# A 512-token, two-layer hybrid model on one core: a reordered key search, gate slabs of sixteen keys, and part of a gate product moved from VectorE to ScalarE

## The chip, the cores and the metric

The kernel runs as one program on one core of a Trainium2 chip. The metric is the device time of an execution in microseconds; less is better. The kernel before was run three times.

## The reference, cut to what matters

The model has two layers over 512 tokens of width 1024 in float32. Each layer is a recurrent mixer, a cross attention and a product-key expert layer ("peer"). The change touches only the last:

```python
def block(hc):                       # D=1024, 8 heads, 2 x 128 keys, 16 chosen
    q = (hc @ wq).reshape(PEER_BLOCK, PEER_HEADS, 2, PEER_DHALF)
    sc = jnp.einsum('thcd,hckd->thck', q, keys)
    s1, i1 = lax.top_k(sc[:, :, 0], 16); s2, i2 = lax.top_k(sc[:, :, 1], 16)
    cand = (s1[..., :, None] + s2[..., None, :]).reshape(..., 256)
    cidx = (i1[..., :, None] * 128 + i2[..., None, :]).reshape(..., 256)
    top, pos = lax.top_k(cand, 16)
    eidx = jnp.take_along_axis(cidx, pos, axis=-1)
    gate = jax.nn.softmax(top, axis=-1)
    act = jax.nn.gelu(jnp.einsum('thkd,td->thk', u_tab[eidx], hc))
    return jnp.einsum('thk,thkd->td', gate * act, v_tab[eidx])
```

## The kernel before

The expert layer is computed densely for 352 tokens (TD) and by gathered rows for the other 160. Dense means: all 16384 experts are visited as 128 tiles of 128 experts. An up tile is 24 matmuls (8 slices of the width, each split into high and low parts and multiplied three times); its result, after gelu, goes to DRAM (`acts`) or stays in SBUF for the last 18 keys. A down tile is the gelu result times a gate matrix, then 24 more matmuls into 8 PSUM banks. TensorE takes the tiles in one fixed order. A tile m is loaded by a DMA that SyncE issues, its high part is made by ScalarE (`split_high`, L216), its low part by VectorE (`split_low`, L221); three tiles can be in flight (NRAW, NSPLIT), and SyncE's loop issues the load of a tile once the low part of the tile three before it is made.

Rows means: GpSimd gathers one expert row per token by indirect DMA (L2564, 128 rows of 4 KB, 0.52 MB), into a ring of six, and VectorE forms the dot product with the token (L2881) or, later, adds the weighted row of the down table (L2887). There are 160 gathers of the up table (ROWS) and 128 of the down table, with 32 more (`part_row`) summed by TensorE.

A layer's peer part has these stages, written out by hand as one program for each engine:
- Search. For each of eight heads VectorE runs `search` (top 16 of the key scores, top 16 of the pair sums `cand`, and the arithmetic that turns a position into two key numbers) while TensorE runs 12 tiles: two query tiles 512 wide and ten up tiles 352 wide, and 16 score matmuls. `split_and_row` puts one low part and, from the second head on, one or two dot rows between the steps of the search; 14 rows per head (ROWS_BY_HEAD). `link` makes VectorE wait for its own last instruction before it starts another.
- Groups. For each of 22 groups of 16 tokens VectorE makes two one-hot planes over the 128 keys (L2991, L2992) and three gate planes (L2994, the gate split into three bfloat16 parts), TensorE multiplies them (`spread_gates`, 48 matmuls, L2618), ScalarE copies the result (`take_gates`, L2737) and SyncE stores it to `gates` in DRAM. One or two up tiles stand between two groups. VectorE adds 0.75 dot rows per group (ROWS_BY_GROUP).
- The last 12 up tiles, with two dot rows each (ROWS_BY_TILE).
- Down. `weigh(e)` multiplies a gelu tile by its gates, which come back in slabs of 8 keys (1.4 MB, two buffers, one DMA each). What is left of the 160 dot rows is spread over the first 8 tiles (DOTS_UNTIL), and the 128 rows of the down table over tiles 10 to 124.

## Time and profile before

| | us |
|---|---|
| median of three runs (3557.41 to 3569.17) | 3567.39 |
| the profiled execution | 3566.76 |
| its span, first to last instruction | 3564.8 |

The share of the span that each engine is busy: TensorE 96%, VectorE 84%, ScalarE 38%, GpSimd 28%. TensorE's mean granted clock is 0.990 of full speed. In the rows below a time is in us from the span's start; a timeline row has start, duration, engine, line, operation, output<-inputs, and in brackets the idle time ahead of it with what ended it. The duration of an instruction on VectorE or ScalarE is longer than the distance to the next start where nothing has to be waited for. A row of busy times has the stretch, its length, then for each engine the busy time (and the number of instructions), and at its end the granted clock of TensorE, the share of DMA engines busy and GB/s.

### The profile page before, as it was taken

The numbers are of one execution on the slowest core, as the hardware profiler recorded it, in microseconds if no ns is written. First come the engines' busy times: TensorE is split into PE (matmuls) and PEld (weight loads), VectorE is DVE, ScalarE is ACT, GpSimd is POOL, SyncE is SP. The second block draws the span as 40 slices with busy tenths as digits, with TensorE's granted clock in tenths as the row PEclk, the third lists the DMA queues.
The fourth block names the chain that finished last, engine by engine and source line by source line (L and its number), as shares of the span: only waits on it lengthen the run. The fifth ranks groups of instructions, "written<-read, shape, count | busy, mean of one in ns | idle before, by whom it ended". The sixth has DMA issues, their size and how long they took to land. (4 is left out here: it accounts for less than half of the span.)

```text
span 3564.8 us, 68150 instructions
## 1 busy us (share of the span) xinstructions
PE 3416.0 (96%) x27550; PEld 3116.0 (87%) x27550; DVE 2986.1 (84%) x5697; ACT 1363.2 (38%) x2116; POOL 989.6 (28%) x756
## 2 busy tenths in 40 slices
PE   8899899999999989999999989999999999999998
PEld 5678677999899989999997877789998999999997
DVE  8687575899999978888888757489999997888887
ACT  3541343433334433333344135343333443333333
POOL 2000000133343245445510000002334324543452
PEclk9999999999999999999999999999999999999999
DMA  7820431699899999999962043259989999999995
GB/s 236 302 95 23 132 113 60 192 292 310 291 358 319 345 336 359 369 376 368 366 220 83 20 121 119 65 155 299 311 297 348 317 349 327 374 383 384 363 367 205
DMA packets 392170, 922.20 MB, mean 259 GB/s; under 512 B 33968, under 2 KB 211248, under 8 KB 385072
## 3 DMA queue, kind: packets, MB, share of 16 engines
q1 hardware_dynamic: 298672, 582.20, 48.7%
q0 software_dynamic: 93184, 335.65, 25.1%
q8 instruction: 217, 3.56, 0.4%
q14 instruction: 97, 0.79, 0.1%
HBM read 802.51 MB, written 113.05 MB: 257 GB/s over the span
## 5 line engine op out<-in xcount | busy, mean ns | idle before, releaser
L2564 POOL DMA_INDIRECT row<-in_peer_u_rows,row_at x320 | 414.6, 1296 | 739.0 <-DVE row L2881 629.3
L228 PE MATMUL peer_ps<-peer_h_high,tile_high 128*128 128x352 f32 (+1 forms) x1504 | 498.0, 331 | 17.0 <-DVE tile_low L221 14.1
L229 PE MATMUL peer_ps<-peer_h_low,tile_high 128*128 128x352 f32 (+1 forms) x1504 | 492.2, 327 | 0.0
L230 PE MATMUL peer_ps<-peer_h_high,tile_low 128*128 128x352 f32 (+1 forms) x1504 | 491.7, 327 | 0.0
L221 DVE TENSOR_TENSOR tile_low<-peer_tile,tile_high 128x1024 fp32r<-128x1024 f32 x362 | 441.4, 1220 | 30.9 <-ACT tile_high L216 27.4
L228 PE MATMUL peer_ps<-gate_high,tile_high 128*128 128x352 f32 x1360 | 442.6, 325 | 9.6 <-DVE tile_low L221 9.3
L230 PE MATMUL peer_ps<-gate_high,tile_low 128*128 128x352 f32 x1360 | 441.3, 325 | 0.0
L229 PE MATMUL peer_ps<-gate_low,tile_high 128*128 128x352 f32 x1360 | 439.5, 323 | 0.0
L216 ACT ACTIVATE tile_high<-peer_tile 128x1024 fp32r<-128x1024 f32 x362 | 379.5, 1049 | 14.1 <-DMA peer_tile<-in_peer_u 14.1
L216 ACT ACTIVATE gate_high<-weighed 128x352 fp32r<-128x352 f32 x256 | 127.8, 499 | 643.6 <-DMA peer_tile<-in_peer_v 332.6
L2881 DVE SCALAR_TENSOR_TENSOR row<-row,h_own 128x1024 f32<-128x1024 f32 x256 | 307.4, 1219 | 23.1 <-DMA row<-in_peer_u_rows,row_at 22.9
L2716 ACT ACTIVATE up_act<-peer_ps 128x352 f32<-128x352 f32 x220 | 102.5, 466 | 575.6 <-PE peer_ps L230 294.1
L228 PEld LDWEIGHTS peer_ps<-peer_h_high,tile_high 128*128 128x128 f32 x1504 | 282.7, 188 | 38.7 <-DVE tile_low L221 23.8
L2564 POOL DMA_INDIRECT late_row<-in_peer_v,row_at x130 | 223.5, 1719 | 239.6 <-DVE h_own L2887 221.1
L230 PEld LDWEIGHTS peer_ps<-peer_h_high,tile_low 128*128 128x128 f32 x1504 | 283.2, 188 | 3.9
L229 PEld LDWEIGHTS peer_ps<-peer_h_low,tile_high 128*128 128x128 f32 x1504 | 283.1, 188 | 3.9
L2564 POOL DMA_INDIRECT row<-in_peer_v,row_at x126 | 215.7, 1712 | 216.3 <-DVE h_own L2887 201.7
L228 PEld LDWEIGHTS peer_ps<-gate_high,tile_high 128*128 128x128 f32 x1360 | 255.3, 188 | 16.0 <-DVE tile_low L221 15.4
L228 PE MATMUL peer_ps<-peer_h_high,peer_tile_high 128*128 128x352 f32 (+1 forms) x736 | 249.9, 339 | 18.0 <-DVE peer_tile_low L221 12.4
L230 PEld LDWEIGHTS peer_ps<-gate_high,tile_low 128*128 128x128 f32 x1360 | 256.3, 188 | 0.0
L229 PEld LDWEIGHTS peer_ps<-gate_low,tile_high 128*128 128x128 f32 x1360 | 255.6, 188 | 0.0
L221 DVE TENSOR_TENSOR gate_low<-weighed,gate_high 128x352 fp32r<-128x352 f32 x256 | 133.0, 520 | 135.2 <-ACT tile_high L216 92.6
(571 smaller groups left out, 8179.0 us busy)
## 6 DMA issues: line engine op xcount, KB each, us to landing
peer_tile<-in_peer_u SPq DMA_DIRECT2D x256, 512.0 KB, 5.4
peer_tile<-in_peer_v SPq DMA_DIRECT2D x256, 512.0 KB, 6.2
gates<-gates_out SPq DMA_DIRECT2D x44, 1024.0 KB, 9.1
gates_in<-gates SPq DMA_DIRECT2D x32, 1408.0 KB, 10.4
acts<-up_act SPq DMA_DIRECT2D x220, 176.0 KB, 5.6
act_in<-acts SPq DMA_DIRECT2D x220, 176.0 KB, 6.1
in_w<-in_w_in SPq DMA_DIRECT2D x32, 512.0 KB, 3.6
peer_tile<-in_peer_wq SPq DMA_DIRECT2D x32, 512.0 KB, 5.1
```

Source lines behind the costliest of these rows:

```text
L216: return act.activation(out, value, ACT.Copy)
L221: return dve.tensor_tensor(out, value, high.bitcast(F32), ALU.subtract)
L228: pe.matmul(out, wh, mh, start=first, stop=False)
L229: pe.matmul(out, wh, ml, start=False, stop=False)
L230: return pe.matmul(out, wl, mh, start=False, stop=last)
L2564: pool.indirect_dma_start(row_of(n)[:, :], None, table, bass.IndirectOffsetOnAxis(ap=row_at[:, row_col(n):row_col(n) + 1], axis=0)) \
L2716: act.activation(up[i % NUP][:, :], ps[m % NPS][:, 0:TD], ACT.Gelu_apprx_tanh).then_inc(taken.sem, 1)
L2881: last = dve.scalar_tensor_tensor(out=x, in0=x, scalar=1.0, in1=(h_own if j < OWN else h_extra)[:, :], op0=ALU.mult, op1=ALU.mult, accum_o ...
```

## The change

- Search. The scans of a head are ordered so that low parts and rows stand behind almost every step: `mark` takes the number of an instruction, `gap` puts low parts and rows there (12 and 16 in 29 shares), and `until` waits for the marked one afterwards. Rows per head go from 14 to 16. The pair blocks become four of 16 pairs and one of a single pair (65 candidates for 64), and the number of a block is found by one shift by four bits, where there were one compare, three compare-and-adds and a cast.
- Groups. Of the third gate plane VectorE multiplies only the first four of eight token pairs (SCALED = 4); ScalarE makes the other eight tokens with eight instructions of 128 elements (`scale_third`), of which it does those of group g+1 between the tiles of group g and `take_gates(g)`, and those of group 0 ahead of both. `spread_gates` waits for them, and so does VectorE before it overwrites the second one-hot plane. Rows per group go from 0.75 to 1.25.
- The last 12 up tiles have one row each, where they had two.
- Slabs hold 16 keys, and are loaded in four pieces at different tiles; the first two loads take a half slab each. The second starts only in the down stage.
- GpSimd's order of gathers follows the new number of rows; its first gather of the down table also waits for the last gate store.

The diff, cut to its core (buffers' places and the counts of semaphores are left out):

```diff
+SCALED = 4
 OWN = PH * TOPK
 ROWS = OWN + PH * EX_COLS
 NROW = 6
 PARTS = 4
 EX_ROUNDS = PH * EX_COLS // PARTS
 BATCH = PH // 2
-ROWS_BY_HEAD, ROWS_BY_GROUP, ROWS_BY_TILE = 14, 0.75, 2.0
+ROWS_BY_HEAD, ROWS_BY_GROUP, ROWS_BY_TILE = 16, 1.25, 1.0
 DOTS_UNTIL = 8
 ROWS_END = NKEY - 4
-PAIRS = ((0, 1, 16), (1, 3, 8), (4, 4, 4), (8, 8, 1))
+PAIRS = ((0, 1, 16), (1, 2, 8), (3, 4, 4), (7, 8, 2), (15, 1, 1))
+GAPS = 29
 PAIR_AT = [sum(some * wide for _, some, wide in PAIRS[:j]) for j in range(len(PAIRS) + 1)]
 PAIRED = PAIR_AT[-1]
 SPILL = GROUP
-SLAB, NSLAB, NACT = 8, 2, 4
+SLAB, NSLAB, NACT = 16, 2, 4
 SLABS = NKEY // SLAB
-KEPT_LATE, KEPT_EARLY = SLAB, 10
+PIECES = ((0, 6), (6, 12), (12, 17), (17, TD // SPILL))
+KEPT_LATE, KEPT_EARLY = SLAB // 2, 10
 KEPT = KEPT_LATE + KEPT_EARLY
 NUP = 3
-DOWN = [s * SLAB + j for s in (*reversed(range(SLABS - -(-KEPT // SLAB), SLABS)), *range(SLABS - -(-KEPT // SLAB))) for j in range(SLAB)]
+TAKEN = [(SLABS - 1, SLAB // 2, SLAB // 2), (SLABS - 1, 0, SLAB // 2), *((s, 0, SLAB) for s in (SLABS - 2, *range(SLABS - 2)))]
+TAKEN_AT = [sum(some for _, _, some in TAKEN[:j]) for j in range(len(TAKEN))]
+DOWN = [s * SLAB + first + j for s, first, some in TAKEN for j in range(some)]
+PIECES_AT = [(0, 2, 4, 5), (4, 5, 6, 7), *([TAKEN_AT[s - 1] + 1 + j for j in ((2, 5, 8, 11) if TAKEN[s - 1][2] == SLAB else (0, 2, 4, 5))]
+                                           for s in range(2, len(TAKEN)))]
...
-PART_GATES_AT = (63, 105)
-PART_GATHER_AT = {42: 0, 79: 1, 88: 2, 96: 3, 108: 4, 111: 5, 114: 6, 117: 7}
+PART_GATES_AT = (71, 119)
+PART_GATHER_AT = {48: 0, 89: 1, 100: 2, 108: 3, 122: 4, 125: 5, 128: 6, 131: 7}
...
-            def load_slab(s):
+            def load_slab(s, piece):
                 if s >= NSLAB:
-                    sp.wait_ge(weighed.sem, weighed.at(SLAB * (s - NSLAB + 1)))
+                    sp.wait_ge(weighed.sem, weighed.at(TAKEN_AT[s - NSLAB + 1]))
+                elif s:
+                    sp.wait_ge(summed.sem, summed.at(UPS))
                 else:
                     for b in range(2):
                         sp.wait_ge(gates_stored[b].sem, gates_stored[b].at(16 * ((TD // SPILL + 1 - b) // 2)))
-                sp.dma_start(slabs[s % NSLAB][:, :, :], gates[DOWN[s * SLAB] // SLAB]) \
+                (at, first, some), groups = TAKEN[s], slice(*PIECES[piece])
+                sp.dma_start(slabs[s % NSLAB][:, groups, 0:some * SPILL], gates[at][:, groups, first * SPILL:(first + some) * SPILL]) \
                     .then_inc(slab_loaded[s % NSLAB].sem, 16)
 
             def load_act(e):
                     store(m - late)
                 if m in gates_at:
                     store_gates(gates_at[m])
-                if m == GROUP_AT[GROUPS] + late + 1:
-                    load_slab(0)
-                if m == UPS:
-                    load_slab(1)
+                if m - GROUP_AT[GROUPS] - late - 1 in PIECES_AT[0]:
+                    load_slab(0, PIECES_AT[0].index(m - GROUP_AT[GROUPS] - late - 1))
             for m in range(UPS + NRAW - late, UPS):
                 store(m)
             for e in range(NRAW, NKEY):
                 if FIRST_LOADED <= e + 2 and DOWN[e + 2:e + 3] and DOWN[e + 2] in LOADED:
                     load_act(LOADED.index(DOWN[e + 2]))
                 load(UPS + e)
-                s = (e - NRAW) // SLAB + NSLAB
-                if (e - NRAW) % SLAB == SLAB - 1 and s < SLABS:
-                    load_slab(s)
+                for s in range(1, len(TAKEN)):
+                    if e in PIECES_AT[s]:
+                        load_slab(s, PIECES_AT[s].index(e))
...
+                    for b in range(2):
+                        pool.wait_ge(gates_stored[b].sem, gates_stored[b].at(16 * ((TD // SPILL + 1 - b) // 2)))
...
+                pe.wait_ge(third_scaled.sem, third_scaled.at(g + 1))
...
+
+            def scale_third(g):
+                act.wait_ge(second_made.sem, second_made.at(g + 1))
+                for h in range(GROUP // 2 - SCALED, GROUP // 2):
+                    for t in range(2):
+                        token = g * GROUP + 2 * h + t
+                        last = act.activation(shares[g % 2][:, PLANES - 1, h, :, t], two[:, h, :, t], ACT.Copy, scale=left[:, token:token + 1])
+                last.then_inc(third_scaled.sem, 1)
...
+                if g == 0:
+                    scale_third(0)
+                if g + 1 < GROUPS:
+                    scale_third(g + 1)
...
-                lows(1)
+            def mark(ins):
+                vec_step.n += 1
+                ins.then_inc(vec_step.sem, 1)
+                return vec_step.n
+
+            def until(step):
+                dve.wait_ge(vec_step.sem, step)
+
+            def lows_of(hd):
+                return BRIDGE + 3 - (PH - 1 - hd) * (UPS_HEAD + 2) - slot_start[0]
+
+            def gap(hd, share):
+                gaps_done[0] += share
+                some = ROWS_BY_HEAD if hd else 0
+                both = (lows_of(hd) + some) * gaps_done[0] // GAPS
+                own_lows = min(both, (2 * lows_of(hd) * gaps_done[0] + GAPS) // (2 * GAPS))
+                lows(slot_start[0] + own_lows - done[0])
                 if hd:
-                    rows((hd - 1) * ROWS_BY_HEAD + ROWS_BY_HEAD * (done[0] - slot_start[0]) // (UPS_HEAD + 2))
-
-            def top16(some, hd):
+                    rows((hd - 1) * ROWS_BY_HEAD + both - own_lows)
+
+            def top16(some, hd, shares):
 
                 for x, r, v, a in some:
                     last = dve.max(v[:, 0:8], x)
-                link(last)
+                best_8 = mark(last)
+                gap(hd, shares[0])
+                until(best_8)
+                for x, r, v, a in some:
+                    last = dve.match_replace(out=r, in_to_replace=v[:, 0:8], in_values=x, imm_value=LOWEST)
+                replaced = mark(last)
                 for x, r, v, a in some:
                     dve.max_index(a[:, 0:8], v[:, 0:8], x)
-                    last = dve.match_replace(out=r, in_to_replace=v[:, 0:8], in_values=x, imm_value=LOWEST)
-                link(last)
-                split_and_row(hd)
+                gap(hd, shares[1])
...
+                gaps_done[0] = 0
                 for two_tb in range(2):
-                    top16([(sc[:, hd % 2, tb, x, :], rest[:, tb, x * NKEY:(x + 1) * NKEY], top[:, tb, x, :], at[:, tb, x, :])
-                           for tb in (2 * two_tb, 2 * two_tb + 1) for x in range(2)], hd)
-                    split_and_row(hd)
-                dve.sem_inc(searched.sem, 1)
+                    if two_tb:
+                        gap(hd, 1)
+                    keys_found = top16([(sc[:, hd % 2, tb, x, :], rest[:, tb, x * NKEY:(x + 1) * NKEY], top[:, tb, x, :], at[:, tb, x, :])
+                                        for tb in (2 * two_tb, 2 * two_tb + 1) for x in range(2)], hd, (2, 2, 2))
                 twins = lambda x: x.rearrange("p t (k a) -> p t k a", a=1).to_broadcast([P, TB, TOPK, 2])
-                dve.tensor_copy(at_first[:, :, :, :], twins(at[:, :, 0, :]))
-                dve.tensor_copy(payload[:, 1, :, :, :], twins(at[:, :, 1, :]))
                 at_pair = 0
                 for first, some, broad in PAIRS:
                     into = cand[:, :, at_pair:at_pair + some * broad].rearrange("p t (a b) -> p t a b", b=broad)
                     last = dve.tensor_tensor(into, down(top[:, :, 0, first:first + some], broad),
                                              across(top[:, :, 1, 0:broad], some), ALU.add)
                     at_pair += some * broad
-                link(last)
-                split_and_row(hd)
-                top16([(cand[:, tb, :], rest[:, tb, 0:PAIRED], best[:, tb, own], pos[:, tb, :])
-                       for tb in range(TB)], hd)
-                split_and_row(hd)
+                paired = mark(last)
+                until(keys_found)
+                dve.sem_inc(searched.sem, 1)
+                dve.tensor_copy(at_first[:, :, :, :], twins(at[:, :, 0, :]))
+                cast = mark(dve.tensor_copy(payload[:, 1, :, :, :], twins(at[:, :, 1, :])))
+                gap(hd, 1)
+                until(paired)
+                pairs_found = top16([(cand[:, tb, :], rest[:, tb, 0:PAIRED], best[:, tb, own], pos[:, tb, :])
+                                     for tb in range(TB)], hd, (2, 1, 2))
+                until(cast)
                 dve.tensor_tensor(payload[:, 0, :, 1:TOPK, :], at_first[:, :, 1:TOPK, :], at_first[:, :, 0:TOPK - 1, :], ALU.subtract)
-                link(dve.tensor_copy(spotf[0][:, :, :], pos[:, :, :]))
-                dve.tensor_copy(payload[:, 0, :, 0:1, :], at_first[:, :, 0:1, :])
-                link(dve.tensor_scalar(spotf[1][:, :, :], spotf[0][:, :, :], float(PAIR_AT[1]), None, ALU.is_ge))
-                link(dve.scalar_tensor_tensor(out=spotf[1][:, :, :], in0=spotf[0][:, :, :], scalar=float(PAIR_AT[2]),
-                                              in1=spotf[1][:, :, :], op0=ALU.is_ge, op1=ALU.add))
-                for _ in range(2):
-                    link(dve.scalar_tensor_tensor(out=spotf[1][:, :, :], in0=spotf[0][:, :, :], scalar=float(PAIR_AT[3]),
-                                                  in1=spotf[1][:, :, :], op0=ALU.is_ge, op1=ALU.add))
-                link(dve.tensor_copy(wide[:, :, :], spotf[1][:, :, :]))
-                link(dve.tensor_tensor(spot[:, :, :], mask[:, :, :], wide[:, :, :], ALU.logical_shift_right))
-                link(dve.tensor_tensor(spot[:, :, :], pos[:, :, :], spot[:, :, :], ALU.bitwise_and))
-                dve.tensor_copy(spotf[1][:, :, :], spot[:, :, :])
-                link(dve.tensor_tensor(hit[:, 0, :, :, :], across(spotf[0][:, :, :], TOPK), every(starts[:, :, :]), ALU.is_ge))
-                split_and_row(hd)
-                link(dve.tensor_tensor(hit[:, 1, :, :, :], across(spotf[1][:, :, :], TOPK), every(ranks[:, :, :]), ALU.is_equal))
+                steps_made = mark(dve.tensor_copy(payload[:, 0, :, 0:1, :], at_first[:, :, 0:1, :]))
+                until(pairs_found)
+                block_known = mark(dve.tensor_tensor(wide[:, :, :], pos[:, :, :], fours[:, :, :], ALU.logical_shift_right))
+                spot_0 = mark(dve.tensor_copy(spotf[0][:, :, :], pos[:, :, :]))
+                until(block_known)
+                masked = mark(dve.tensor_tensor(spot[:, :, :], mask[:, :, :], wide[:, :, :], ALU.logical_shift_right))
+                until(spot_0)
+                dve.tensor_tensor(hit[:, 0, :, :, :], across(spotf[0][:, :, :], TOPK), every(starts[:, :, :]), ALU.is_ge)
+                until(masked)
+                spot_1 = mark(dve.tensor_tensor(spot[:, :, :], pos[:, :, :], spot[:, :, :], ALU.bitwise_and))
+                gap(hd, 1)
+                until(spot_1)
+                spot_1 = mark(dve.tensor_copy(spotf[1][:, :, :], spot[:, :, :]))
+                gap(hd, 1)
+                until(spot_1)
+                hit_1 = mark(dve.tensor_tensor(hit[:, 1, :, :, :], across(spotf[1][:, :, :], TOPK), every(ranks[:, :, :]), ALU.is_equal))
+                gap(hd, 1)
+                until(hit_1)
                 pairs = hit[:, :, :, :, :].rearrange("p j t a (k c) -> p (j t a) k c", c=2)
-                link(dve.tensor_tensor(pairs, pairs, payload[:, :, :, :, :].rearrange("p j t (a k) c -> p (j t a) k c", k=1)
-                                       .to_broadcast([P, 2 * TB * TOPK, TOPK // 2, 2]), ALU.mult))
-                split_and_row(hd)
+                hits_known = mark(dve.tensor_tensor(pairs, pairs, payload[:, :, :, :, :].rearrange("p j t (a k) c -> p (j t a) k c", k=1)
+                                                    .to_broadcast([P, 2 * TB * TOPK, TOPK // 2, 2]), ALU.mult))
                 summed_hits = hit
                 for into in hits:
+                    gap(hd, 1)
...
+                    dve.wait_ge(third_scaled.sem, third_scaled.at(g))
+                dve.tensor_tensor(two[:, :, :, :], keys_at, per_key(1), ALU.is_equal).then_inc(second_made.sem, 1)
                 link(dve.tensor_tensor(one[g % 2][:, :, :, :], keys_at, per_key(0), ALU.is_equal))
                 for j in range(PLANES):
-                    last = dve.tensor_tensor(shares[g % 2][:, j, :, :, :], two[:, :, :, :], per_key(2 + j), ALU.mult)
+                    some = slice(0, GROUP // 2 - SCALED * (j + 1 == PLANES))
+                    last = dve.tensor_tensor(shares[g % 2][:, j, some, :, :], two[:, some, :, :], per_key(2 + j)[:, some, :, :], ALU.mult)
...
-                for _ in range(BRIDGE + 3 - (PH - 1 - hd) * (UPS_HEAD + 2) - done[0]):
-                    split_and_row(hd)
-                rows(hd * ROWS_BY_HEAD)
...
-                dve.wait_ge(slab_loaded[s % NSLAB].sem, slab_loaded[s % NSLAB].at(16 * (s // NSLAB + 1)))
+                dve.wait_ge(slab_loaded[s % NSLAB].sem, slab_loaded[s % NSLAB].at(16 * len(PIECES) * (s // NSLAB + 1)))
                 by = lambda x: x.rearrange("p (g t) -> p g t", t=SPILL)
                 dve.tensor_tensor(by(mixed[e % 2][:, :]), by(value),
-                                  slabs[s % NSLAB][:, :, (e % SLAB) * SPILL:(e % SLAB + 1) * SPILL], ALU.mult).then_inc(weighed.sem, 1)
+                                  slabs[s % NSLAB][:, :, (e - TAKEN_AT[s]) * SPILL:(e - TAKEN_AT[s] + 1) * SPILL], ALU.mult).then_inc(weighed.sem, 1)
...
```

## Rows read from the trace of the kernel before

**Rows 1.** The page's first section: busy time, share, instructions.

```profile
PE 3416.0 (96%) x27550; PEld 3116.0 (87%) x27550; DVE 2986.1 (84%) x5697; ACT 1363.2 (38%) x2116; POOL 989.6 (28%) x756
```

**Rows 2.** Busy time by stretch: search, groups, last up tiles, down; first and second layer.

```profile
691.00:1092.80 401.80, 390.42 (x2322) 367.74 (x2320) 381.15 (x1191) 142.88 (x206) 155.51 (x139) 1.00 0.92 314
1092.80:1273.40 180.60, 180.21 (x1809) 169.65 (x1809) 174.93 (x174) 84.21 (x146) 50.45 (x31) 1.00 1.00 324
1273.40:1333.50 60.10, 48.97 (x292) 47.81 (x289) 42.78 (x65) 18.76 (x29) 34.68 (x25) 0.96 0.97 357
1333.50:1420.00 86.50, 83.56 (x492) 81.54 (x492) 77.06 (x112) 30.06 (x44) 45.56 (x30) 0.97 0.97 362
1420.00:1851.00 431.00, 424.61 (x2614) 420.84 (x2613) 363.84 (x447) 159.91 (x221) 203.38 (x110) 1.00 0.93 349
...
2976.40:3035.50 59.10, 48.54 (x291) 47.67 (x288) 42.41 (x65) 18.49 (x29) 36.30 (x25) 0.97 0.97 364
3035.50:3120.00 84.50, 82.16 (x482) 80.67 (x483) 76.86 (x112) 29.64 (x43) 48.66 (x30) 0.96 0.99 372
3120.00:3546.70 426.70, 424.35 (x2624) 422.59 (x2622) 365.40 (x446) 157.34 (x218) 180.64 (x111) 1.00 0.92 350
```

**Rows 3.** The same view over 100 us in the middle of the second down stage.

```profile
3200.00:3300.00 100.00, 100.00 (x619) 100.00 (x619) 89.05 (x107) 37.57 (x52) 36.10 (x29) 1.00 1.00 382
```

**Rows 4.** Who waited for whom in 1273.4 to 1333.5: sum, times, longest.

```profile
DVE row L2881 <- DMA row<-in_peer_u_rows,row_at: 11.7, 9, 3.9
ACT tile_high L216 <- DMA peer_tile<-in_peer_u: 11.2, 4, 5.2
...
PE peer_ps L228 <- DVE peer_tile_low L221: 7.7, 2, 4.4
```

**Rows 5.** Timeline: the score matmuls of a head and two 512-wide matmuls on TensorE.

```profile
872.23 1.95 PE L2606 MATMUL peer_ps<-keys,queries 128*128 128x128 f32 x16
...
1852.67 0.39 PE L229 MATMUL front_ps<-front_x_low,front_tile_high 128*128 128x512 f32 x1
1852.90 0.40 PE L230 MATMUL front_ps<-front_x_high,front_tile_low 128*128 128x512 f32 x1
```

**Rows 6.** Timeline of VectorE: the first scans of two successive heads.

```profile
907.45 0.86 DVE L2849 MAX8 key_top<-key_scores 128x8 f32<-128x128 f32 x4
...
960.41 0.87 DVE L2849 MAX8 key_top<-key_scores 128x8 f32<-128x128 f32 x4
```

**Rows 7.** Timeline of VectorE: a step with a link behind it, then instructions without.

```profile
892.27 1.23 DVE L2931 TENSOR_TENSOR hit<-hit,pair_payload 128x2048 bf16<-128x2048 bf16 x1
893.53 1.23 DVE L221 TENSOR_TENSOR tile_low<-peer_tile,tile_high 128x1024 fp32r<-128x1024 f32 x1
894.68 1.22 DVE L2881 SCALAR_TENSOR_TENSOR row<-row,h_extra 128x1024 f32<-128x1024 f32 x1
```

**Rows 8.** Timeline of VectorE: first and last of the steps that find the block.

```profile
886.71 0.17 DVE L2917 TENSOR_SCALAR spotf<-spotf 128x64 bf16<-128x64 bf16 x1
...
887.92 0.23 DVE L2924 TENSOR_TENSOR spot<-pair_mask,pair_wide 128x64 uint32<-128x64 uint32 x1
```

**Rows 9.** VectorE, grouped by shape: a gate plane, and half its elements.

```profile
L2994 DVE TENSOR_TENSOR onehot_gates<-onehot_second,route 128x2048 bf16<-128x2048 bf16 x57 | 66.4, 1220 | 0.6
...
L2929 DVE TENSOR_TENSOR hit<-spotf,pair_ranks 128x1024 bf16<-128x1024 bf16 x8 | 5.5, 686 | 0.0
```

**Rows 10.** Timeline: TensorE's first gate product, and ScalarE around it.

```profile
1092.79 2.93 PE L2618 MATMUL peer_ps<-onehot_gates,onehot 128*128 128x128 bf16 x48 [0.86 <-DVE onehot_gates L2994]
...
1093.10 1.05 ACT L216 ACTIVATE tile_high<-peer_tile 128x1024 fp32r<-128x1024 f32 x1
1094.05 2.31 ACT L2737 ACTIVATE gates_out<-peer_ps 128x512 f32<-128x512 f32 x4
```

**Rows 11.** Timeline of ScalarE: an instruction of 128 elements.

```profile
1368.23 0.31 ACT L2815 ACTIVATE row_dots<-row_dots 128x128 f32<-128x128 f32 x1 [3.53 <-DVEq L3121]
```

**Rows 12.** Timeline: one of TensorE's waits in the down stage.

```profile
1446.93 0.43 PE L228 MATMUL peer_ps<-gate_high,peer_tile_high 128*128 128x352 f32 x1 [1.37 <-DVE peer_tile_low L221]
```

49 lines of the change are left out of this document (30 added, 19 removed).

## The prediction

> **What bounds the kernel now.** I read the page's first section, then the busy times by stretch, then the waits, then single timelines. TensorE is busy 96% of the span [rows 1], so all that can be won is the time in which it is held up, and a stretch where it is not held up gives nothing, whatever the other engines do. The busy times by stretch say where it is held up [rows 2]: idle TensorE is 401.8 - 390.4 = 11.4 us in the search, 0.4 us in the groups, 11.1 us in the last twelve up tiles, 2.9 and 6.4 us in the down stage. The second layer has about the same. A busy TensorE can still be slow, so I also set up floors. Where nothing disturbs it, 100 us hold 620 matmuls of 352 columns (619 are recorded) [rows 3], 0.161 us each, 3.86 us a tile.
> - Last up tiles: 12 x 3.86 = 46.4 us against 60.1 and 59.1 us. Lost: 13.7 and 12.7.
> - Down: 3072 x 0.1613 = 495.5, and some 3 us for the last small products, say 499, against 86.5 + 431.0 = 517.5 and 84.5 + 426.7 = 511.2. Lost: 18.5 and 12.2.
> - Search, per head: 240 x 0.16 = 38.4, the two query tiles 48 x 0.23 = 11.0, the scores about 1.8 [rows 5], so 51.2 us. The distance of two heads on VectorE is 52.96 us [rows 6], and the whole stretch has 11.4 us of idleness. Lost: about 12, in each layer.
> - Groups: nothing lost. VectorE is busy 174.9 of 180.6 us beside it, so two engines are full at once.
> Together 44 and 37 us, 81 us for both layers: no version of this change can win more.
>
> **What holds it up.** In the search VectorE is busy 381 of 402 us [rows 2]: it is the bound, and low parts come late behind long runs of scans. In the last up tiles it is the transfers: VectorE waits 11.7 us for gathered rows, ScalarE 11.2 us for up tiles, and TensorE then for low parts [rows 4]. The bytes say why: 12 tiles and 24 rows of 0.52 MB, two slabs of 1.44 and a gate store of 1.05 are 22.8 MB; at the floor's 46.4 us that is 490 GB/s, and the stretch moved 357 to 364 [rows 2]. In the down stage single waits of about 1 us come at about the pace of the slab loads [rows 12].
>
> **The change part by part.** The sum is made against the profiled execution's 3566.8 us (span 3564.8 and 2.0 around it), which lies 0.6 us below the median of the runs.
>
> Search. A linked step costs more than its work: the row after a link starts 1.26 us after a 1.23 us instruction, while two instructions without a link are 1.15 us apart, one of 1.23 and one of 1.22 us [rows 7]; so a link costs 0.11 us. A head has 29 links. Five go with the removed steps, and of the other 24 about 22 get a low part, a row or an independent step between, as 28 items are spread over 29 shares: 22 x 0.11 = 2.4 us. The removed steps run from 886.71 to 887.92, 1.2 us with their links [rows 8]. The shift and the fifth pair block come in, at about 0.13 us each (a 0.23 us step less what overlaps) 0.3 us. Two more rows cost 2 x 1.145 = 2.3 us. VectorE per head: -2.4 -1.2 +0.3 +2.3 = -1.0 us, to 51.9, close above TensorE's 51.2. Seven heads have rows, so 7 us; the first head, without new rows, is bound by TensorE. Even spacing of the low parts should take some of the single waits away, yet two more gathers per head add 1.05 MB in 53 us, 20 GB/s, to the 314 that the search moves with its DMA engines busy 0.92 [rows 2]. I take 6 us gained per layer; the bounds are 10 (nearly all that is lost, the floor binding) and a loss of 4 (as with the last up tiles, the late transfers return as waits).
> The Trainium skill, page "VectorE: DVE Perf Modes", section "Rules for kernel authors", says that chained VectorE instructions drain in any case, so that one should cut their number and not their semaphores. These rows differ from it: 1.26 against 1.15 us. By the page the 2.4 us would not come, VectorE would have 1.4 us more per head, and the search would lose about 10 us a layer.
>
> Groups. VectorE saves half a plane: 1.22 - 0.69 = 0.53 us per group [rows 9], 11.7 us in 22. It gains 27 - 16 = 11 rows, 12.6 us. Net +0.9 us, on an engine that has 5.7 us of room over the stage [rows 2]: hidden. If that room were gone it would cost the 0.9. ScalarE gets eight instructions of 128 elements, 0.31 us each alone [rows 11] and about 0.2 apart, 1.7 us a group; the upper bound is that they overlap in nothing and cost as a 352-wide one, 0.5 us, 4 us a group. ScalarE is busy 84.2 of 180.6 us, 3.8 of 8.2 per group, so 1.7 fits. Behind `scale_third` in its queue stand `take_gates` and the next tile's high part; the wait for the second plane is short, since that plane is VectorE's first step of the group and ends 4.6 us ahead of the last. One place has no cover: in group 0 `scale_third(0)` stands after the tile's high part, which ends at about 1094.05, while TensorE's first product now starts at 1092.79 after 0.86 us of waiting [rows 10]. It would start at 1094.05 + 1.7 = 1095.8: 3.0 us lost per layer (bounds 2 and 5). VectorE's wait for the same instructions before group 1 costs it some 2 us, which are covered by TensorE's own delay. Bigger stores (1 KB pieces for 512 B) and 11 more gathers stand against each other on DMA engines that are full here (1.00) [rows 2]; I take zero, from -1 to +2.
> The same skill, page "ScalarE: Activation LUTs", section "What ACT_TABLE_LOAD costs", gives about 93 ns more for an operand that is a pointer per partition, as this scale is. No row here has one of that form alone. By it the eight cost 2.5 us, and the first product comes 0.8 us later still.
>
> Last up tiles. 12 rows less, 6.3 MB, and the second slab's 1.44 MB go out: 22.8 - 7.7 = 15.1 MB in 46.4 us are 325 GB/s, below the 357 to 364 that the stretch has moved and below 382 [rows 3]. So the stage falls to its floor, with 2 us left: 11.7 and 10.7 gained (bounds 7, half of it, and all 13). The last piece of the first slab is issued for tile 144, two tiles or 7.7 us before VectorE wants it, about as long as a landing under load; VectorE's own lead over TensorE of some 4 us is the cover, and without it 1 to 2 us would be lost.
>
> Down, first 20 tiles. 160 - 142 = 18 dot rows are left before, 2.25 a tile; after, 98 + 14 + 4 + 27 + 12 = 155 are done and five are left. VectorE per tile goes from 0.44 + 0.44 + 1.14 + 2.25 x 1.145 = 4.6 us, above TensorE's 3.86, to 2.7. The loss there is 2.9 us of idleness and 0.03 x 86.5 = 2.6 us of clock at a granted 0.97 [rows 2]; I take 4 gained of these 5.5 (bounds 2 and 5). The second slab's last piece comes in tile 7 and is wanted for weigh(8), again two tiles.
> Down, the rest. The bytes are the same; bursts of 1.44 MB become pieces of 0.65 to 0.79 MB every three tiles. The idle time is 6.4 us in the first layer and 2.4 in the second [rows 2]. I take 3 and 1 (bounds 0, and all of it).
>
> Sum. First layer: 6 - 3 + 11.7 + 4 + 3 = 21.7. Second: 6 - 3 + 10.7 + 4 + 1 = 18.7. Together 40.4 us: 3566.8 - 40.4 = **3526.4**, and 3527 against the median.
>
> **The rivals.**
> A. The search is bound by transfers. For it: a DMA share of 0.92 already [rows 2]. Against it: the last down stage ran at 382 GB/s with TensorE full [rows 3]. It loses 4 us per layer instead of gaining 6: 3526 + 20 = 3546.
> B. The last up tiles are not freed, since pieces of the slab and the two small slack times take over: half of the gain, 2 x 5.6 = 11, and down tiles give 2 x 2 less: 3541.
> C. Links cost nothing, so that only the number of steps counts (the first skill rule). The search loses 10 instead of gaining 6: 3526 + 32 = 3558. Against it stands the 0.11 us of [rows 7].
> D. Slower: ScalarE becomes the bound of the groups. In a group with one tile TensorE needs 3.9 + 2.8 = 6.7 us; ScalarE needs 1.3 for the tile, 2.0 for the copies [rows 10] and eight scalings. From 0.42 us per scaling on it is the later one in 14 of 22 groups, and `spread_gates` waits each time; at 0.6 us it is 1.5 us x 14 = 21, with the waits for gate stores that its idle time now absorbs some 30 us a layer: 3526 + 60 = 3586. It decides against the change from about 0.55 us on. The 0.31 us row speaks against it [rows 11].
> E. More than forecast: the search reaches its floor and the down stage loses no more: 3526 - 2 x 4 - 7 = 3511.
>
> **How the numbers follow.** Forecast 0.50, A 0.14, B 0.11, C 0.07, D 0.07, E 0.11. The forecast's own range, with its bounds combined, is 3512 to 3543. To hold 8 in 10 the range takes in B, most of E and most of A with their bounds: 3502 to 3555. A measurement of this kernel can tell about 0.3%, 11 us, from no change. Faster by more than that (below 3556.7) are the forecast, B, E and four fifths of A: 0.83. The same: 0.10, from C and the end of A. Slower: 0.07, D.
>
> **What would show it.** The groups' stretch grows by 3 us, with one TensorE wait for ScalarE at its start, and no such wait in later groups. The last up tiles take 47 to 50 us, and VectorE's waits for gathered rows are gone there. The head distance on VectorE is 52 us or less, with 16 rows in it. The scalings last 0.3 to 0.4 us each. DMA in the search is at 335 to 345 GB/s. It would be wrong if ScalarE's waits for stores of `acts` reach TensorE in the search, or if the down stage's first ten tiles wait for slab pieces.

## The result, and the profile after

The changed kernel takes 3526.5 us (median of four runs, 3523.3 to 3528.3) where the kernel before, run beside it, takes 3564.4: a ratio of 0.989, 95% interval 0.987 to 0.991. The forecast was 3527, faster. Yet only the sum was right: several of its terms were off by about their own size or more, and the errors cancelled. That the total came out within 2 us is luck. So the experiments ask of each term whether its mechanism is there and what it is worth.

The span of the profiled execution is 3525.9 us (3564.8 before). These are the changed kernel's busy times by stretch, in the columns of [rows 2], each stretch beginning with TensorE's same instruction: first to last score product of the first layer (a part of the next line's stretch); search and the way to the first gate product; groups, last twelve up tiles and down stage of the first layer, then the last two stages of the second layer.

```profile
647.40:978.90 331.50, 327.75 (x1945) 311.40 (x1944) 315.87 (x1065) 124.20 (x180) 121.50 (x105) 1.00 0.88 300
690.00:1099.90 409.90, 395.75 (x2356) 374.70 (x2355) 380.91 (x1200) 148.87 (x218) 178.70 (x154) 0.99 0.94 330
1099.90:1284.00 184.10, 182.13 (x1809) 171.56 (x1810) 175.78 (x196) 130.91 (x313) 64.30 (x42) 0.99 0.94 337
1284.00:1330.30 46.30, 46.30 (x289) 46.30 (x289) 30.68 (x43) 18.10 (x28) 15.10 (x12) 1.00 0.97 354
1330.30:1831.60 501.30, 501.07 (x3105) 500.69 (x3103) 428.64 (x529) 189.91 (x264) 173.39 (x128) 1.00 0.93 349
2959.90:3006.20 46.30, 46.30 (x290) 46.30 (x289) 30.58 (x43) 18.29 (x28) 15.86 (x12) 1.00 0.97 352
3006.20:3507.30 501.10, 500.95 (x3105) 500.76 (x3104) 428.00 (x528) 186.85 (x260) 160.48 (x128) 1.00 0.93 348
```

The last up tiles and the down stage are at their floors in both layers: TensorE (second and third number) is busy with hardly a gap. The groups are longer than the 180.6 of [rows 2] although ScalarE (fifth number) has taken work from VectorE. And the way to the first gate product (second line) is longer than the 401.8 of [rows 2], where the forecast had it shorter.

To see where, I took the starts of the same TensorE instructions in both traces: the eight score products of a layer, the first gate product, the end of the groups, the first down tile. Times in us, first / second layer; every experiment was read in the same way.

| kernel | first to last score | to first gate product | groups | last up tiles | down |
|---|---|---|---|---|---|
| before | 338.6 / 336.9 | 111.4 / 113.0 | 180.8 / 180.5 | 59.9 / 59.0 | 517.5 / 510.8 |
| after | 331.5 / 331.3 | 121.0 / 118.8 | 184.0 / 185.8 | 46.3 / 46.3 | 501.2 / 501.0 |
| difference | -7.1 / -5.6 | +9.6 / +5.8 | +3.2 / +5.3 | -13.6 / -12.7 | -16.3 / -9.8 |
| after, run again | 328.5 / 329.2 | 119.8 / 120.7 | 184.4 / 183.4 | 46.3 / 46.3 | 501.0 / 501.0 |

The differences add up to -24.2 and -17.0, -41.2 us in all. The spans differ by 38.9, since the rest of the program is 2.3 longer: the first score product, ahead of which nothing is changed, starts at 647.4 and not at 642.8, and over all kernels here between 638.8 and 647.4. In the two executions of the changed kernel the first three columns differ by up to 3 us, the last two by 0.2.

Where TensorE now waits, by the view of its waits over the whole span (us in total, times, longest):

```profile
PE peer_ps L2631 <- ACT onehot_gates L2759: 11.1, 2, 6.0
PE peer_ps L228 <- ACT up_act L2729: 9.7, 12, 1.7
PE peer_ps L2631 <- DVE onehot_gates L3056: 4.9, 2, 3.0
PE peer_ps L228 <- DVE peer_tile_low L221: 4.8, 2, 3.0
```

The first row is ScalarE's scaling in group 0, once a layer, and is new. The second is TensorE waiting for ScalarE's activations in the search; the kernel before has such waits too:

```profile
PE peer_ps L228 <- ACT up_act L2716: 7.3, 6, 2.1
```

The third is a VectorE wait in the middle of the groups, once a layer. The fourth comes just ahead of group 0.

### The profile page after: what moved, and what is told of

Read it like the earlier page. It is cut to its first block and busy times, and to the rows that moved or that the text cites. A ratio compares the mean times of both kernels' runs of the same rounds, so it can differ in the third digit from the quotient of the medians.

```text
span 3525.9 us, 68362 instructions
## 1 busy us (share of the span) xinstructions
PE 3398.6 (96%) x27550; PEld 3112.3 (88%) x27550; DVE 2928.4 (83%) x5651; ACT 1463.5 (42%) x2468; POOL 877.6 (25%) x756
## 5 line engine op out<-in xcount | busy, mean ns | idle before, releaser
L2576 POOL DMA_INDIRECT row<-in_peer_u_rows,row_at x320 | 403.9, 1262 | 564.7 <-DVE row L2927 437.2
L228 PEld LDWEIGHTS peer_ps<-peer_h_high,tile_high 128*128 128x128 f32 x1504 | 282.7, 188 | 30.5 <-issue 18.7
L229 PE MATMUL peer_ps<-peer_h_low,peer_tile_high 128*128 128x352 f32 (+1 forms) x736 | 244.8, 333 | 0.0
L230 PE MATMUL peer_ps<-peer_h_high,peer_tile_low 128*128 128x352 f32 (+1 forms) x736 | 244.5, 332 | 0.0
```

What stands on the lines that cost most here:

```text
L228: pe.matmul(out, wh, mh, start=first, stop=False)
L229: pe.matmul(out, wh, ml, start=False, stop=False)
L230: return pe.matmul(out, wl, mh, start=False, stop=last)
L2576: pool.indirect_dma_start(row_of(n)[:, :], None, table, bass.IndirectOffsetOnAxis(ap=row_at[:, row_col(n):row_col(n) + 1], axis=0)) \
```

## The experiments

All ratios are to the kernel before on the same chip, with 95% intervals.

**The changed kernel again**, to have it beside the others.

> The changed kernel unchanged, as the mark for the other kernels of this set: both theories expect 0.989 of the kernel before, some 38 us less.

3522.9 us, ratio 0.988 [0.985, 0.991].

**The waits between linked steps put back.** The order of the search stays as it is.

```diff
                 ins.then_inc(vec_step.sem, 1)
+                dve.wait_ge(vec_step.sem, vec_step.n)
                 return vec_step.n
```

> The changed kernel, but every marked step of the search is waited for at once, as a link does, with order, rows and slabs as in the changed kernel. Theory: a wait for the last instruction costs 0.11 us, some 22 to 24 per head, 2.5 us a head on a VectorE that is the bound: the distance of two heads grows from about 52.5 to 54 or 55 us and the kernel is 20 to 35 us slower than the changed one. Rival (the rule that waits cost nothing and only the number of instructions counts): within 4 us of the changed one.

3560.2 us, 0.999 [0.997, 1.000]: nearly the whole gain is gone, 37 us of it against the changed kernel run again, a little more than the 20 to 35 expected. First to last score takes 347.1 / 344.1 us, 15.6 and 12.8 more than after (18.6 and 14.9 against its second execution). The first two of the seven distances from score to score, 16.7 and 51.1 us, are the same in both kernels, so all of it falls in the other five. VectorE's first scans of successive heads, from the second head on, stand 3.0 and 2.6 us further apart on average. The way to the first gate product grows by another 4 to 5. TensorE waits for VectorE's low parts again, as the view of its waits over the whole span says (the changed kernel has 1.8 us of this row, in 4 waits):

```profile
PE peer_ps L228 <- DVE tile_low L221: 26.4, 22, 2.4
```

So a wait of VectorE for its own last instruction is not free: 2.6 to 3.0 us for the 27 marks of a head are 0.10 to 0.11 us each, the forecast's 0.11 (it had counted 22 such waits). Rival C falls. With it, for this kernel, falls the rule of the Trainium skill, page "VectorE: DVE Perf Modes", section "Rules for kernel authors", by which one should cut the number of chained instructions and not their semaphores: here the number stayed and the semaphores cost 37 us.

**Rows put back, the rest of the change kept**, and **rows alone moved in the kernel before**. The part gates and part gathers that go with the rows are moved too.

```diff
-ROWS_BY_HEAD, ROWS_BY_GROUP, ROWS_BY_TILE = 16, 1.25, 1.0
+ROWS_BY_HEAD, ROWS_BY_GROUP, ROWS_BY_TILE = 14, 0.75, 2.0
...
-PART_GATES_AT = (71, 119)
-PART_GATHER_AT = {48: 0, 89: 1, 100: 2, 108: 3, 122: 4, 125: 5, 128: 6, 131: 7}
+PART_GATES_AT = (63, 105)
+PART_GATHER_AT = {42: 0, 79: 1, 88: 2, 96: 3, 108: 4, 111: 5, 114: 6, 117: 7}
```

The second kernel is the opposite edit in the kernel before.

> The changed kernel, but with the rows spread as before: 14 per head, 0.75 per group, 2 per last up tile, and GpSimd's part gathers at the places that go with it. Theory: the stalls of the last up tiles and of the first down tiles came from the transfers of 24 and 18 rows there, so the last twelve tiles go from 46.3 back to 56 to 60 us with VectorE waiting for gathered rows, the down stage from 501 to 504 to 508, while search and groups win some 4 us a layer: 20 to 35 us slower than the changed kernel. Rival: the slab pieces and their places freed these stages: the last up tiles stay below 50 us and the time within 8 us of the changed one.

> The kernel before, with nothing of the change but the spread of the rows (16, 1.25, 1) and the part gathers' places. Theory: the last up tiles fall to 47 us as in the changed kernel, but two more rows per head (2.3 us) and 11 more in the groups (12.6 us) fall on a VectorE without room, so search and groups grow by about 13 and 7 us a layer and eat the gain: 0.995 to 1.006 of the kernel before. Rival: the spread alone brings most of the change's gain, below 0.993.

Rows back: 3551.5 us, 0.996 [0.995, 0.998], within the 20 to 35 us expected. Rows alone: 3570.8 us, 1.001 [1.000, 1.002], as expected.

| kernel | first to last score | to first gate product | groups | last up tiles | down |
|---|---|---|---|---|---|
| rows back | 325.9 / 325.7 | 117.2 / 115.5 | 182.2 / 181.8 | 60.1 / 59.5 | 516.1 / 513.0 |
| rows alone | 347.8 / 346.5 | 116.4 / 116.9 | 190.7 / 193.9 | 46.0 / 46.3 | 504.0 / 502.5 |

The stretches from first to last score, last up tiles and down of rows back:

```profile
645.40:971.30 325.90, 325.84 (x1946) 311.55 (x1945) 304.86 (x1046) 124.02 (x180) 115.99 (x96) 1.00 0.85 288
1270.70:1330.80 60.10, 48.71 (x289) 47.55 (x287) 42.27 (x64) 18.10 (x29) 32.69 (x25) 0.95 0.96 344
1330.80:1846.90 516.10, 506.54 (x3104) 505.19 (x3104) 445.07 (x558) 190.00 (x264) 178.08 (x140) 0.99 0.94 353
```

and of rows alone, the groups, last up tiles and down:

```profile
1110.60:1301.30 190.70, 182.86 (x1809) 171.41 (x1810) 187.34 (x196) 84.10 (x145) 68.19 (x42) 0.99 0.99 327
1301.30:1347.30 46.00, 46.00 (x289) 46.00 (x289) 29.05 (x41) 18.36 (x28) 17.25 (x12) 1.00 1.03 396
1347.30:1851.30 504.00, 501.99 (x3106) 500.66 (x3104) 430.27 (x530) 190.24 (x265) 184.34 (x128) 1.00 0.92 345
```

Three readings. The 13 us stall of the last up tiles follows the rows alone: it returns with two rows per tile although the slab comes in pieces, and goes with one row although whole slabs stay. The new search order with 14 rows has TensorE busy 325.84 of 325.90 us, its floor; it is worth 12.7 and 11.2 us. The two added rows per head then cost 5.6 us a layer (2.6 and 3.5 if the second execution of the changed kernel is taken); in the old order they cost 9.2 and 9.6. And rows alone give nothing: what they free late (13.9 and 12.7 in the last up tiles, 13.5 and 8.3 in the down stage) they cost early (14 and 14 to the first gate product, 10 and 13 in the groups). The new search order makes them payable; what the scalings add is asked below. The down stage of rows back is worse than the 504 to 508 expected: nearly all of its loss, 15.0 us in the first layer, falls in its first 50 us, against 6.6 us there in the kernel before.

What the two rows cost in the search shows in ScalarE's waits there, the changed kernel first, from first to last score:

```profile
ACT up_act L2729 <- DMA acts<-up_act: 91.6, 28, 6.4
```

and rows back:

```profile
ACT up_act L2729 <- DMA acts<-up_act: 47.1, 12, 6.0
```

With the new order, ScalarE waits about twice as long for the buffers that the stores of `acts` give back, and some of it reaches TensorE: of the 5.6 us, TensorE's idle time is 3.7, and 3.1 of it waits for ScalarE's activations. But the number of rows alone does not set these waits. The kernel before, with 14 rows and the old order, has

```profile
ACT up_act L2716 <- DMA acts<-up_act: 84.5, 26, 6.6
```

DMA moves 300 GB/s in that stretch of the changed kernel, 288 in rows back, at a share of 0.88 and 0.85. So the DMA engines are not full on average; I read it as stores landing later among more gathers, but no run separates that from another cause.

**Group 0 left to VectorE.** ScalarE's scalings begin with group 1.

```diff
-                pe.wait_ge(third_scaled.sem, third_scaled.at(g + 1))
+                if g:
+                    pe.wait_ge(third_scaled.sem, third_scaled.at(g))
...
-                if g == 0:
-                    scale_third(0)
...
-                    dve.wait_ge(third_scaled.sem, third_scaled.at(g))
+                if g >= 2:
+                    dve.wait_ge(third_scaled.sem, third_scaled.at(g - 1))
...
-                    some = slice(0, GROUP // 2 - SCALED * (j + 1 == PLANES))
+                    some = slice(0, GROUP // 2 - SCALED * (j + 1 == PLANES and g > 0))
```

> The changed kernel, but VectorE makes the whole third plane of group 0, and TensorE, VectorE and ScalarE wait for scalings from group 1 on. Theory: the one uncovered place of the moved work is group 0, where TensorE waits 5.1 and 6.0 us for ScalarE and then runs at a lower granted clock; without it these waits fall below 1 us, the first gate product starts 5 us earlier, and the kernel is 10 to 16 us faster than the changed one (5 to 6 us and about 2 us of clock per layer). Rival: VectorE is as late as ScalarE there, so the wait only changes its name, and less than 4 us are won.

3513.1 us, 0.984 [0.981, 0.987], 10 us below the changed kernel, at the lower end of the 10 to 16 expected. The way to the first gate product is 114.4 / 115.9, 6.6 and 2.9 us less (5.4 and 4.8 against the second execution); the groups take 186.0 / 186.6.

How eight short instructions come to cost more than the 3.0 us of the forecast is seen in the changed kernel's timeline (start, us, engine, line, operation; in brackets the wait just before and what ended it):

```profile
1076.49 1.23 DVE L2927 SCALAR_TENSOR_TENSOR row<-row,h_extra 128x1024 f32<-128x1024 f32 x1 [3.15 <-DMA row<-in_peer_u_rows,row_at]
1085.27 0.43 PE L228 MATMUL peer_ps<-peer_h_high,peer_tile_high 128*128 128x352 f32 x1 [2.96 <-DVE peer_tile_low L221]
1093.63 0.47 ACT L2729 ACTIVATE up_act<-peer_ps 128x352 f32<-128x352 f32 x1 [9.88 <-DMA acts<-up_act]
1097.30 2.47 ACT L2759 ACTIVATE onehot_gates<-onehot_second,gates_left 128x128 bf16<-128x128 bf16 x8
1099.87 1.23 DVE L3052 TENSOR_TENSOR onehot_second<-key_ramp,route 128x2048 bf16<-128x2048 bf16 x1 [5.08 <-ACT onehot_gates L2759]
1099.91 4.57 PE L2631 MATMUL peer_ps<-onehot_gates,onehot 128*128 128x128 bf16 x48 [5.11 <-ACT onehot_gates L2759]
```

VectorE waits 3.15 us for a gathered row, low parts come late and TensorE waits 2.96; ScalarE has waited 9.88 us for a store of `acts` when it makes its last activation; only behind that come the eight scalings, at 1097.30, and they last 2.47 us, not 1.7. TensorE waits 5.11 us and VectorE 5.08. A late activation alone is not what the forecast missed, for the kernel before has it in the same place:

```profile
1091.20 0.46 ACT L2716 ACTIVATE up_act<-peer_ps 128x352 f32<-128x352 f32 x1 [6.86 <-DMA acts<-up_act]
```

Counted from the moment when TensorE has done its tiles (1091.93 before, 1094.80 after), the forecast's scalings would begin 2.1 us later and last 1.7, a wait of 3.8. Here they begin 2.5 us later and the product follows after another 2.6: 5.1. In the second layer they begin 3.4 us later, and the wait is 6.0:

```profile
2774.12 5.28 PE L2631 MATMUL peer_ps<-onehot_gates,onehot 128*128 128x128 bf16 x48 [6.01 <-ACT onehot_gates L2759]
```

Behind these waits the 48 products take 4.57 and 5.28 us, where they took 2.93 and 2.92 before: 1.6 and 2.4 us more, which the table counts among the groups. In the same place the kernel without group 0's scalings:

```profile
1088.42 2.47 ACT L2760 ACTIVATE onehot_gates<-onehot_second,gates_left 128x128 bf16<-128x128 bf16 x8
1086.36 2.92 PE L2632 MATMUL peer_ps<-onehot_gates,onehot 128*128 128x128 bf16 x48
1207.53 4.50 PE L2632 MATMUL peer_ps<-onehot_gates,onehot 128*128 128x128 bf16 x48 [2.66 <-DVE onehot_gates L3056]
```

The first gate product starts with no wait (1.03 us in the second layer), and the scalings (of group 1 now) run beside it. The third line is the VectorE wait in the middle of the groups: it stays, is longer than the changed kernel's 1.96, and the products behind it are slow now. That is why the groups do not get shorter although their first product does.

**The whole third plane on VectorE**, in every group, with rows and all else as changed.

```diff
-SCALED = 4
+SCALED = 0
...
-                pe.wait_ge(third_scaled.sem, third_scaled.at(g + 1))
...
-                if g == 0:
-                    scale_third(0)
-                if g + 1 < GROUPS:
-                    scale_third(g + 1)
...
-                    dve.wait_ge(third_scaled.sem, third_scaled.at(g))
```

> The changed kernel, but VectorE makes the whole third plane of every group, and nobody waits for ScalarE's scalings. Theory: VectorE gets 0.57 us per group, 12 us a layer, with some 5 us of room, so the groups grow to 188 to 192 us from their first product on while the wait of 5 us ahead of it is gone: 0 to 8 us slower than the changed kernel and 10 to 18 slower than group0_on_vector. Rival: VectorE has the room after all, the offload brings nothing, and the kernel is as fast as group0_on_vector.

3524.0 us, 0.988 [0.986, 0.991]: the time can't be told from the changed kernel's, and is 11 us above group 0 alone on VectorE, both as expected. The first gate product comes 5.0 and 2.2 us sooner (116.0 / 116.6), and the groups are longer by 8.2 and 3.9:

```profile
1085.70:1277.90 192.20, 182.54 (x1809) 171.11 (x1810) 187.38 (x196) 84.37 (x146) 67.13 (x42) 0.99 0.94 324
```

VectorE is busy 187.4 of 192.2 us: it is the bound. With the results above this makes a square for the groups, first / second layer:

| | plane on VectorE | half of it on ScalarE |
|---|---|---|
| 0.75 rows a group | 180.8 / 180.5 (before) | 182.2 / 181.8 (rows back) |
| 1.25 rows a group | 192.2 / 189.7 (this), 190.7 / 193.9 (rows alone) | 184.0 / 185.8 (after) |

At 0.75 rows the scalings only lose, 1.4 us, which is the slower products behind group 0's wait (4.92 and 4.48 us there); beside the added rows they give 4 to 8. (The kernels of a line differ in search order and slabs as well, which end or begin outside the groups; slabs of 16 keys are also stored in larger pieces within them, and no run takes that apart.) The 10 us of group 0 take about all of it back. So as written the scalings bring nothing, and the changed kernel's whole gain is there without them; begun with group 1 they do bring something.

**The scaling without its pointer operand.** The half of the third plane that ScalarE makes is copied and not multiplied.

```diff
-                        last = act.activation(shares[g % 2][:, PLANES - 1, h, :, t], two[:, h, :, t], ACT.Copy, scale=left[:, token:token + 1])
+                        last = act.activation(shares[g % 2][:, PLANES - 1, h, :, t], two[:, h, :, t], ACT.Copy, scale=1.0)
```

> The changed kernel, but ScalarE's eight scalings multiply by the constant 1.0 and not by the token's remainder of the gate, so this part of the gates is wrong; everything else is done. It is there for the price of the operand. The forecast's sum (from a 128-element instruction of 0.31 us) expects the same duration with the per-partition operand as without; the Trainium skill's page ScalarE: Activation LUTs expects about 0.09 us less per instruction here, so eight of them 1.8 us where the changed kernel shows 2.47.

Groups of instructions by line and form, in a stretch of the groups; the changed kernel first (shape, count, busy, mean ns of one, idle time before them and its cause), then this one:

```profile
L2759 ACT ACTIVATE onehot_gates<-onehot_second,gates_left 128x128 bf16<-128x128 bf16 x149 | 46.3, 430 | 8.2 <-DVE onehot_second L3052 8.2
```

```profile
L2759 ACT ACTIVATE onehot_gates<-onehot_second 128x128 bf16<-128x128 bf16 x144 | 31.4, 342 | 6.8 <-DVE onehot_second L3052 6.8
```

430 against 342 ns: the pointer costs 88 ns. The Trainium skill, page "ScalarE: Activation LUTs", section "What ACT_TABLE_LOAD costs", says about 93 for each such operand; the trace agrees. From it the prediction had estimated 2.5 us for eight, and they take 2.47, against 1.75 to 1.78 here (1.8 expected). The row that I had used is of float32 elements and a constant scale [rows 11]. The kernel's time, 3525.5 in its only run, can't be told from the changed kernel's.

**Whole slabs.** A slab of sixteen keys is loaded at once, two halves first.

```diff
-PIECES = ((0, 6), (6, 12), (12, 17), (17, TD // SPILL))
+PIECES = ((0, TD // SPILL),)
...
-PIECES_AT = [(0, 2, 4, 5), (4, 5, 6, 7), *([TAKEN_AT[s - 1] + 1 + j for j in ((2, 5, 8, 11) if TAKEN[s - 1][2] == SLAB else (0, 2, 4, 5))]
+PIECES_AT = [(0,), (4,), *([TAKEN_AT[s - 1] + 1 + j for j in ((2,) if TAKEN[s - 1][2] == SLAB else (0,))]
```

> The changed kernel, but each slab of gates comes in one transfer (1.4 MB for the two half slabs, 2.9 MB for the others), issued where the first piece was. Theory: the waits at slab loads in the down stage before came from bursts, so with bursts twice the size the down stage goes from 501 us to 508 to 515 and the kernel is 10 to 25 us slower than the changed one. Rival: the down stage was freed by the rows that are gone from its start, and a transfer asked for this early disturbs nobody: within 4 us.

3557.4 us, 0.998 [0.996, 0.999]: with whole slabs nearly all of the gain is gone, 31 to 35 us where 10 to 25 were expected, since the last up tiles suffer as well. Last up tiles and down stage of the first layer, by stretch, then the new wait of TensorE in the last up tiles, and ScalarE's wait for an up tile ahead of it (us in total, times, longest):

```profile
1281.20:1335.10 53.90, 48.62 (x289) 48.34 (x289) 30.41 (x43) 17.91 (x28) 16.61 (x12) 0.94 0.86 305
1335.10:1846.10 511.00, 503.66 (x3105) 500.41 (x3104) 427.63 (x529) 189.92 (x264) 194.26 (x128) 1.00 0.92 343
```

```profile
1317.44 0.66 PE L228 MATMUL peer_ps<-peer_h_high,tile_high 128*128 128x352 f32 x1 [5.28 <-DVE tile_low L221]
ACT tile_high L216 <- DMA peer_tile<-in_peer_u: 10.1, 1, 10.1
```

7.6 and 5.2 us come back in the last up tiles, 9.8 and 10.6 in the down stage. DMA moves 343 GB/s here and 349 in the changed kernel's down stage, so it is not the bytes. It is single tiles that come late: ScalarE's longest wait for an up tile in the last up tiles is 10.1 us, 0.6 in the changed kernel, and for a down tile 9.0 against 5.7. With sixteen-key slabs the pieces carry these 33 us. In the kernel with rows alone, where slabs hold eight keys and come whole, the last up tiles are free and the down stage loses only 3.0 and 1.5 us to the 501. So the pieces mostly pay for what the larger slab would cost; against whole slabs of eight keys, larger slabs and pieces together have 4.5 us to win in these stages.

**Three mends together.** Group 0 on VectorE, the last low parts of the search ahead of the rows, and one of GpSimd's part gathers three rows later, away from the wait of VectorE in the middle of the groups.

```diff
-PART_GATHER_AT = {48: 0, 89: 1, 100: 2, 108: 3, 122: 4, 125: 5, 128: 6, 131: 7}
+PART_GATHER_AT = {48: 0, 89: 1, 100: 2, 108: 3, 122: 4, 125: 5, 128: 6, 134: 7}
...
+            lows(1)
+            rows(searched_rows + 2)
+            lows(1)
             rows(searched_rows + 4)
             dve.wait_ge(flip_taken.sem, flip_taken.at(TB - 1))
-            lows(2)
```

> The changed kernel with three changes: group 0's third plane on VectorE; the two low parts ahead of the gate flips are made between and before the four rows there; the last gather of part rows stands ahead of row 134, where it stood ahead of row 131. Theory: the first saves 6 to 8 us a layer, the second the waits of 3.0 and 1.9 us with the clock behind them, 2 to 4 a layer, the third the waits of 2.0 and 3.0 us at the gate product of the fifteenth group: 20 to 28 us in all, near 3502. Rival: the transfers of acts set the pace there, and a mended wait returns a few us later: less than 14 us.

3510.7 us, 0.983 [0.979, 0.987], against 0.984 with group 0 alone: the other two give nothing that can be told. It is 12 us below the changed kernel, not 20 to 28; the rival had said less than 14. The wait that the moved gather was to remove, in the changed kernel's timeline:

```profile
1197.71 1.89 POOL L2550 DMA_INDIRECT part_row<-in_peer_v,row_at  x1 [14.74 <-PE peer_ps L2641]
1205.73 1.44 POOL L2576 DMA_INDIRECT row<-in_peer_u_rows,row_at  x1 [0.31 <-issue]
1214.09 1.22 DVE L2927 SCALAR_TENSOR_TENSOR row<-row,h_own 128x1024 f32<-128x1024 f32 x1 [6.04 <-DMA row<-in_peer_u_rows,row_at]
1220.65 2.93 PE L2631 MATMUL peer_ps<-onehot_gates,onehot 128*128 128x128 bf16 x48 [1.96 <-DVE onehot_gates L3056]
```

GpSimd's gathers go out in order in this trace: its part gather waits 14.74 us for TensorE, the row's gather stands behind it, and VectorE waits 6.04 us for that row. With the gather moved this is gone, and in its place stands another:

```profile
1183.30 2.07 ACT L2751 ACTIVATE gates_out<-peer_ps 128x512 f32<-128x512 f32 x4 [5.36 <-DMA gates<-gates_out]
1184.04 4.37 PE L2632 MATMUL peer_ps<-onehot_gates,onehot 128*128 128x128 bf16 x48 [3.23 <-ACT gates_out L2751]
```

ScalarE waits for gate stores and TensorE for ScalarE. That is the rival's mechanism, with gate stores in place of stores of `acts`. The groups take 186.6 / 186.8 us, as before the mend.

**Fewer rows in the search.** Group 0 on VectorE, and 15 or 14 rows per head; the ones left go to the down stage, where `DOTS_UNTIL` spreads them over 12 or 16 tiles instead of 8.

```diff
-ROWS_BY_HEAD, ROWS_BY_GROUP, ROWS_BY_TILE = 16, 1.25, 1.0
-DOTS_UNTIL = 8
+ROWS_BY_HEAD, ROWS_BY_GROUP, ROWS_BY_TILE = 14, 1.25, 1.0
+DOTS_UNTIL = 16
```

> group0_on_vector with 15 rows per head for 16, so that 12 of the 160 rows are left for the down stage, spread over its first 12 tiles (1.0 a tile, with TensorE's 3.86 us a tile against 0.44 + 0.44 + 1.14 + 1.15 = 3.2 on VectorE). Theory: two more rows per head than 14 cost the search about 1 us a head in waits of ScalarE for stores, so 15 wins half of it, 3 us a layer, and the down stage stays at 501: 4 to 8 us faster than group0_on_vector, near 3506. Rival: any row asked for in the early down stage brings its stalls back (11 to 15 us a layer with 18 rows in 8 tiles): slower by 5 us or more.

> group0_on_vector with 14 rows per head as before, 19 left for the down stage and spread over its first 16 tiles (1.2 a tile). Theory: the search runs at its floor of 51.1 us a head, 5 us a layer less, and the down stage stays within 2 us of 501, as it is the two rows a tile and not rows as such that its transfers cannot carry: 6 to 12 us faster than group0_on_vector, near 3503. Rival: as for rows_15, slower by 5 us or more.

With 15: 3500.6 us, 0.981 [0.979, 0.983]. With 14: 3499.9 us, 0.980 [0.978, 0.983]. The two can't be told apart and are the fastest here, 23 to 27 us below the changed kernel and some 13 below group 0 alone, a little more than the 4 to 8 and 6 to 12 expected. With 14 the search is at its floor again:

```profile
643.70:970.30 326.60, 326.11 (x1946) 311.58 (x1945) 306.00 (x1048) 124.09 (x180) 110.61 (x95) 1.00 0.85 289
```

Part gates and part gathers are moved with the rows in both. The way to the first gate product is 112.9 / 112.2, and the down stage stays at 501.0 / 501.8 with the rows it has taken.

## Why the prediction was right, point by point

**Search.** Forecast: 6 us gained a layer. Measured from first to last score: 7.1 and 5.6 (10.1 and 7.7 in the second execution). The price of a link is confirmed by putting the waits back. The pair of heads in [rows 6] moved as forecast; its `MAX8` groups start at

```profile
906.81 0.86 DVE L2889 MAX8 key_top<-key_scores 128x8 f32<-128x128 f32 x4
958.82 0.87 DVE L2889 MAX8 key_top<-key_scores 128x8 f32<-128x128 f32 x4
```

52.0 us apart (52.96 in [rows 6]; 51.9 forecast). But one pair is not the search. The six distances from the second head on average 53.3 and 53.2 us (53.7 and 53.4 before), so that the sign "52 us or less" did not come true, and another 4 us come from the first head (33.0 us for 36.9), which the forecast had held to be bound by TensorE. The sum's two sides were both too large: it had 3.3 us a head from the order, 23 in seven heads, and 2.3 a head for the rows, 16. By the runs the order gives 12.7 and 11.2, where it meets TensorE's floor, and the rows take 3 to 6 back. Their balance came out near 6; that is in part luck. The sign against the forecast, ScalarE's waits for stores that reach TensorE, is there with 3.1 us, but the kernel before has 2.5 us of it in the same stretch, so it separates nothing; rival A's loss did not come. DMA moves 330 GB/s to the first gate product, below the 335 to 345 named.

**The way from the last score to group 0** had no term of its own but the 3.0 us of group 0. It grew by 9.6 and 5.8 us. TensorE's wait at the first gate product grew from 0.86 to 5.11 and from 0.81 to 6.01 us: 4.3 and 5.2 of it. With the slower products behind it, group 0 cost 5.9 and 7.6 us, above the bound of 5. The mis-sized term is "1094.05 + 1.7 = 1095.8": the eight instructions take 2.47 us and not 1.7, for the pointer operand; they begin 0.4 and 1.3 us later behind TensorE's last tile than in the old trace; and the clock behind the wait was put at nothing. The run with group 0 on VectorE takes 6.6 and 2.9 off the way. Of the 3.0 and 2.9 that are left, 3.8 and -0.6 stand with 15 rows, 1.5 and -0.8 with 14, and 2.8 and -0.2 with three mends: fewer rows help, but with up to 3 us between executions the cause of this remainder stays open.

**Groups.** Forecast: nothing beside group 0, bounds -1 to +2. Measured: 3.2 and 5.3 longer, counted from the first product's start. "Net +0.9 us, hidden" counted VectorE's busy time right (175.78 against 174.9 in [rows 2]). The growth is two things that the forecast had at nothing: the slower products behind group 0's wait, 1.6 and 2.4 us, and one wait for a late row at the fifteenth group, 1.96 and 2.98 (in the first layer a wait of 0.39 is gone). Together they are 3.2 and 5.3. The second execution agrees, with 2.2 and 1.3 of clock and waits of 1.87 and 1.75 for a growth of 3.6 and 2.9. The sign that the groups would grow by 3 us came true for another reason than the one given: it stood for group 0's wait, which lies ahead of this stretch. No ScalarE scaling holds TensorE up in later groups; rival D is out: the eight take 2.47 us, 0.31 each, where it needed 0.42 to begin and 0.55 to decide, and ScalarE is busy 130.9 of 184.1 us. A single one lasts 0.43, above the 0.3 to 0.4 named; they overlap.

**Last up tiles.** Forecast 11.7 and 10.7, measured 13.6 and 12.7: the mechanism is shown by two runs, the stage reaches its floor of 46.3, and the 2 us kept in reserve were not needed. The lead of two tiles for a slab's last piece was enough, which rival B doubted.

**Down stage.** Forecast 7 and 5, measured 16.3 and 9.8. The floor of 499 is 501 in practice. Both terms were too small, as they were read from idle time [rows 2] and took little for the slower products behind it. In the kernel before, TensorE does 269 products in the first 50 us of either layer where 310 fit, so it is 6.6 us behind, and 9.7 and 3.2 later. Over the first 20 tiles that makes some 7 us a layer, above the bound of 5, where 4 was taken. Nor do the terms simply add. Rows alone, with whole slabs of eight keys, already bring 13.5 and 8.3 of the 16.3 and 9.8, later losses included, and leave 3.0 and 1.5 for slabs and pieces, near the 3 and 1 forecast. Rows back, with pieces, loses nothing after its first 50 us either. So the later loss needed both the crowded start and the whole slabs; how the one works on the other stays open. That a burst costs more than the wait it leaves in the record fits the fall of the clock shown below, but was not measured apart.

**The sum.** From the first score product to the end of the groups the forecast had 3 us a layer gained, and 5.7 and 5.5 were lost: 8.7 and 8.5 worse. The last up tiles and the down stage had 18.7 and 15.7, and gave 29.9 and 22.5: 11.2 and 6.8 better. The errors, 17.2 us one way and 18.0 the other, left 0.8. Their signs agree with one reading, that I priced late transfers too low on both sides, in what bursts had cost and in what the new rows would cost; but no run tests the two as one cause, and part of the early loss is group 0's wait and the clock behind it.

## What to carry to other kernels

When late work is spread forward, price it by the stage that receives it: here rows alone changed nothing, and paid only once the search order had made room. Work handed to another engine should begin with the second item of a pipeline, not the first, where nothing covers it: here the help was worth nothing until it did. A head distance read from one pair of heads is not the stage; take all of them. A wait of an engine for its own last instruction has a price, so put independent work behind each step; and break a large load beside a steady stream into pieces.

## What the runs showed of the hardware

A scaling by a pointer operand takes 430 ns for 128 elements, by a constant 342; the first was not expected from the 0.31 us row. And a wait of TensorE can cost more than itself. The changed kernel around its first gate product, in ten-microsecond windows (in the columns of [rows 2]):

```profile
1085.00:1095.00 10.00, 9.54 (x48) 9.24 (x48) 9.62 (x12) 1.37 (x2) 1.93 (x1) 0.83 0.82 298
1095.00:1105.00 10.00, 5.09 (x56) 4.71 (x60) 5.09 (x5) 7.69 (x23) 0.00 (x0) 0.66 0.27 74
1105.00:1115.00 10.00, 10.00 (x101) 8.73 (x91) 9.97 (x12) 5.06 (x14) 7.14 (x5) 1.00 0.75 234
```

The granted clock has a mean of 0.83 and 0.66 in the first two, between the two levels of 1.2 and 2.4 GHz (0.5 and 1.0 of full speed), around waits of 2.96 and 5.11 us, and is back at 1.00 in the next window. The 48 gate products behind the 5.11 us take 4.57 us, where the same 48 take 2.93 behind 0.86 us in the kernel before: 1.64 us on top. But not every such wait does this. In the second layer of the same kernel a wait of 2.98 us is followed by products at full speed:

```profile
2896.63 2.93 PE L2631 MATMUL peer_ps<-onehot_gates,onehot 128*128 128x128 bf16 x48 [2.98 <-DVE onehot_gates L3056]
```

and in the kernel with group 0 on VectorE one of 2.66 us is followed by 4.50. What decides between the two, these runs don't show.
